# Experts' down weights laid out with two neighbouring lines of the matrix in each partition

## The chip, the cores and the metric

The kernel runs on one core of one Trainium2 chip. Its time is the device time in microseconds (us) of one launch, and a version is judged by the median of its runs. All data are float32.

## What is computed

Two transformer blocks follow each other over 256 tokens of width 1024. The first block has two layers; the second of these ends in a mixture of experts, which is where the change lies. Cut to that part, the reference is:

```python
N_EXPERTS, TOP_K, FFN_EXPERT, MOE_BLOCK = 8, 2, 3584, 128

def moe_swiglu(x, w_router, w1, w3, w2):
    logits = jnp.einsum('nd,de->ne', xf, w_router)
    top_logits, top_idx = lax.top_k(logits, TOP_K)
    gates = jax.nn.softmax(top_logits, axis=-1)
...
    def expert_block(args):
        xb, e = args
        h = jax.nn.silu(xb @ w1[e]) * (xb @ w3[e])
        return h @ w2[e]
```

Each of the eight experts has two up matrices `w1[e]` and `w3[e]` of 1024 x 3584 and a down matrix `w2[e]` of 3584 x 1024. A block of up to 128 tokens (`xb`) meets each expert. In `h @ w2[e]` the sum runs over the 3584 lines of `w2[e]`; the order in which these lines are added is free, as long as line r of the matrix meets column r of `h`.

## The kernel before

**The ring of weights.** All weights stream from the chip's memory through `ring_data`, a ring of 6 slots (`RING`, L33) of 128 partitions x 8 KB, so 1 MB a slot. SyncE (SP) issues the transfers in the order of use, two of 512 KB for each slot, and before each slot it waits until TensorE has used up the slot that lay there (`ring.used`, L716). For each slot that has landed, ScalarE (ACT) rounds the 2048 values of each partition to the format of the fast float32 matmul (`weights_hi`, `e_high`, L2124), VectorE (DVE) subtracts that from the original (`weights_lo`, `e_low`, L2443), and TensorE (PE) makes three products from them: high by high, low by high, high by low. ACT and DVE work three slots ahead of PE (`Wide.LEAD`, L245).

**A turn.** One turn is one expert, 42 slots in a fixed order (`Wide.TURN`, L244): the hidden width of 3584 is cut into chunks of 1024, 1024, 1024 and 512 columns; a chunk takes 8 up slots (4 for the last) and 4 down slots (2 for the last), and the first chunk of the next expert is computed in the turn before (`next`). There are eight turns here: 336 slots, of which 8 x 14 = 112 are down slots. The loop over turns and the lists of slots are the same for SP (`turn_of`), ACT, DVE and PE (`turn`).

**An up slot** holds 128 lines of `w1` and 128 of `w3`, 1024 columns each: every partition gets a run of 4 KB from each (L720). For the last chunk it holds 256 lines of 512 columns, in runs of 2 KB. **A down slot** holds 256 lines of `w2`, each 1024 columns or 4 KB long. Before the change the first transfer brings lines 0 to 127 of the 256, one to each partition, and the second brings lines 128 to 255 (L718 to L720). So partition p holds lines p and 128 + p, and the runs are 4 KB long over all 128 partitions.

**The matmuls.** `up_slot` (L1485, L1486, L1489) and `down_slot` (L1512, L1513, L1517) each issue 12 matmuls of 128 x 512. Line f of the two in a partition meets `ehT[:, 2m + f]` (L1512, L1513), which is the transposed hidden activation: `eh`, 128 tokens x up to 1024 columns, is turned in blocks of 128 x 128 by `turn_h` (L1473), and block q holds columns 128q to 128q + 127. ACT and DVE copy the turned blocks out of PSUM (L2147, L2907). `turn_h` is called four times a turn, with 8, 8, 8 and 4 blocks.

In the rows, `ring_data<-in_moe_w` is a transfer of the experts' weights, `weights_hi` and `weights_lo` are the two halves of a split, and `hT_hi`, `hT_lo` are the turned activations. `arena` is a large buffer in which many tiles lie, `eh` among them. L195 is the line that issues the transfers of all other weights.

Of the kernel before, what the change touches and what calls it, by code (L numbers as in the profile page):

```python
# [14 lines left out]
P = 128  # L15
# [12 lines left out]
CHUNK = 64  # L28
FFN = 2816
E, FE = 8, 3584  # L30
# [257 lines left out]
def cols(ap, c, w):  # L288

    return ap[:, c:c + w].rearrange("(k p) c -> p k c", p=P)  # L290


def two_block_kernel(nc, a, out):

    CO, CONST_W = constant_offsets()
    with ExitStack() as ctx:
# [28 lines left out]
        def sem(name):  # L325

            if name not in S:
                S[name] = ctx.enter_context(nc.semaphore(name))
            return S[name]
# [3 lines left out]
        def bk(i, *dims):  # L333

            n = int(np.prod(dims))
            v = bank[i][:, 0:n]
            if len(dims) == 2:
                v = v.rearrange("p (a b) -> p a b", a=dims[0])
            if len(dims) == 3:
                v = v.rearrange("p (a b c) -> p a b c", a=dims[0], b=dims[1])  # L340
            return v
# [7 lines left out]
        def const(name, k=0, w=None):  # L349
            o, width = CO[name]  # L350
            w = w or width
            return consts[:, o + k * w:o + (k + 1) * w]

        ident, ones, half = const("ident"), const("ones"), const("half")
# [266 lines left out]
        esil, eh = (t.rearrange("p a j c -> p (a j c)") for t in bufs1[:2])  # L621
        ehT_hi, ehT_lo = (t.rearrange("p a q t -> p (a q t)").rearrange("p (k t) -> p k t", k=DT) for t in bufs1[2:])

        def e_slot(at):
            return (n_moe + at) % RING
# [34 lines left out]
        def _(sp):  # L660
# [51 lines left out]
            w1, w3, w2 = (a[k].rearrange("o e d f -> (o e d) f") for k in ("moe_w1", "moe_w3", "moe_w2"))  # L712

            def expert_slot(kind, c, m, e, at, more):

                sp.wait_ge(ring.used, n_moe + at + 1 - RING + more)  # L716
                slot, loaded = ring_data[:, e_slot(at), :], ring.loaded[e_slot(at)]
                if kind == "down":  # L718
                    src = w2[bass.ds(e * FE + 1024 * c + 256 * m, 256), :].rearrange("(f p) d -> p f d", p=P)
                    parts = [(slot.rearrange("p (f d) -> p f d", f=2)[:, i:i + 1, :], src[:, i:i + 1, :]) for i in range(2)]  # L720
                elif c < 3:
                    parts = [(slot[:, 1024 * i:1024 * i + 1024], w[bass.ds(e * D + P * m, P), 1024 * c:1024 * c + 1024]) for i, w in enumerate((w1, w3))]
                else:
                    parts = [(slot[:, 1024 * i:1024 * i + 1024].rearrange("p (k c) -> p k c", k=2),
                              w[bass.ds(e * D + 2 * P * m, 2 * P), 3072:3584].rearrange("(k p) c -> p k c", p=P)) for i, w in enumerate((w1, w3))]
                for d, r in parts:
                    sp.dma_start(d, r).then_inc(loaded, 16)

            def turn_of(it, is_last):
                for s, (kind, c, m) in enumerate(Wide.slots(is_last)):  # L730
                    expert_slot(kind, c, m, (it + (kind == "next")) % E, e_first + s, it * MOE_LOADS)

            for m in range(e_first):
                expert_slot("up", 0, m, 0, m, 0)
# [14 lines left out]
            for m, (c, w, kind) in enumerate(PROJ2):  # L749
                n = N_PROJ2 + m  # L750
                src = cols(a["w_in_2"][0], c, w) if kind != "ki" else None
                if kind == "ki":
                    src = tuple(cols(a["w_in_2"][0], C_KI, HD) for _ in range(2))
                if kind == "kvw":
                    src = (cols(a["w_in_2"][0], C_KV, P), cols(a["w_in_2"][0], C_KI + HD, IH))
                ring2.load(sp, n, ring2.slot(n)[:, 0:8 * w].rearrange("p (k c) -> p k c", k=DT), src)
            for t in range(GATE_SLOTS):
                c, half = C_G + 512 * (t // 2), t % 2
# [6 lines left out]
            for m in range(4):  # L765
                d, rows = m // 2, slice(512 * (m % 2), 512 * (m % 2) + 512)
# [215 lines left out]
        def _(pe):  # L982
# [440 lines left out]
            def moe():  # L1423
                for j in range(TT):
                    for k in range(DT):
                        if j == 0 and k % 2 == 0:
                            pair_arrived(5, k // 2)
                        i = mm(bank[4][:, E * j:E * j + E], actT[:, k, P * j:P * j + P], router_sb[:, k, :], start=k == 0, stop=k == DT - 1)
# [41 lines left out]
                def turn_h(c):  # L1470

                    for q in range(Wide.WIDTHS[c] // P):
                        i = nc.tensor.transpose(bk(6 + q // 4, 4, P)[:, q % 4], eh[:, P * q:P * q + P], ident)  # L1473
                    i.then_inc(sem("moe_hT_psum"), 1)

                def up_slot(c, m, at, split):
# [43 lines left out]
                def turn(it, is_last):  # L1520
                    for s, (kind, c, m) in enumerate(Wide.slots(is_last)):
# [7 lines left out]
                        if part == ("up", 1, 1):  # L1529
                            turn_h(0)  # L1530
# [8 lines left out]
                        if part == ("up", 2, 1):  # L1539
                            pe.wait_ge(sem("y_added"), it * 4 + 4)  # L1540
                            turn_h(1)
# [9 lines left out]
                        if part == ("up", 3, 1):  # L1551
                            pe.wait_ge(sem("pgT_ready"), it + 2)
                            pe.wait_ge(sem("gslot_ready"), it + 1)
                            turn_h(2)
# [1738 lines left out]
```

## Time and profile before

| What | us |
|---|---|
| Median of three runs (lowest to highest) | 2177.38 (2173.64 to 2178.76) |
| Profiled execution, its own time | 2174.22 |
| Its span, first to last instruction | 2172.4 |
| PE busy in the span | 2119.5 (98%) |
| DVE busy | 1595.0 (73%) |
| ACT busy | 1215.9 (56%) |
| Mean rate of all transfers | 250 GB/s |

The span is cut into stages by the work: two mixers and a dense feed-forward part up to some 550 us, the experts from there to some 1557 us, and the second block after that. The hardware profiler's records say for every engine when it worked and for every idle time what ended it. Matmuls overlap each other in the records, so a group's mean duration is longer than the step from one start to the next. "Share of DMA" is the part of the time in which the core's 16 transfer engines had a packet in work.

### The profile page before, as it was taken

To read this page: it belongs to the slowest core of one execution; us is meant where nothing else is said; L and a number is where in the kernel's file an instruction comes from. 1 tells how busy PE (TensorE), PEld (TensorE's weight loads), DVE (VectorE), ACT (ScalarE), POOL (GpSimd) and SP (SyncE) were. 2 spreads that over 40 slices of the span, in tenths; PEclk is the share of its full clock that TensorE was granted. 3 is DMA by queue.
4 is the path that set the end of the run, shared out by engine and by line. 5 is a ranking of instruction groups with operands and counts; after the bars stand their busy time and mean duration, and the time that the engine had idled before them with its cause. 6 is when DMAs were issued, how large, how long until landed. Compare 5 with 4: busy or idle time off the path is not lost.

```text
span 2172.4 us, 31475 instructions
## 1 busy us (share of the span) xinstructions
PE 2119.5 (98%) x11887; PEld 1770.4 (81%) x11887; DVE 1595.0 (73%) x1654; ACT 1215.9 (56%) x1204; POOL 171.3 (8%) x240
## 2 busy tenths in 40 slices
PE   8999999999899999999999999999999999999998
PEld 7987888898778788888888888888788887877886
DVE  3677454577788989989898989989866539776453
ACT  4254443415467777777777777777664423664442
POOL 1200000310200000000000000000166010000000
PEclk9999999999999999999999999999999999999999
DMA  9224555422589999999999999999846564435552
GB/s 353 70 98 165 186 186 184 142 66 93 177 325 373 351 371 375 357 377 360 372 362 371 360 376 367 363 375 362 317 155 192 183 182 156 155 107 173 180 188 78
DMA packets 244114, 542.21 MB, mean 250 GB/s; under 512 B 20182, under 2 KB 122624, under 8 KB 243648
## 3 DMA queue, kind: packets, MB, share of 16 engines
q1 hardware_dynamic: 238608, 521.37, 66.5%
q0 software_dynamic: 4448, 13.79, 2.4%
q10 hardware_dynamic: 976, 5.91, 0.7%
q8 instruction: 57, 0.93, 0.2%
q14 instruction: 25, 0.20, 0.0%
HBM read 538.64 MB, written 2.36 MB: 249 GB/s over the span
## 4 chain that ended last, share of the span: by engine, by line
PE 83%; DVE 10%; issue 3%; ACT 2%; DMA 2%; DVEq 0%; SPq 0%; ACTq 0%
PE bank L1334 9%; PE bank L1335 9%; PE bank L1336 9%; PE bank L1489 7%; PE bank L1485 7%; PE bank L1486 7%; PE bank L1060 6%; PE bank L1512 4%; PE bank L1513 4%; PE bank L1517 4%; DVE weights_lo L2443 2%; PE bank L1058 2%; PE bank L1647 2%; DMA ring_data<-in_moe_w 1%; PE bank L1473 1%
## 5 line engine op out<-in xcount | busy, mean ns | idle before, releaser
L2443 DVE TENSOR_TENSOR weights_lo<-ring_data,weights_hi 128x2048 fp32r<-128x2048 f32 x336 | 760.0, 2288 | 84.4 <-ACT weights_hi L2124 83.2
L2124 ACT ACTIVATE weights_hi<-ring_data 128x2048 fp32r<-128x2048 f32 x336 | 639.0, 1919 | 178.6 <-DMA ring_data<-in_moe_w 178.1
L1485 PE MATMUL bank<-weights_hi,xg_hi 128*128 128x512 f32 x896 | 352.5, 393 | 2.6 <-DVE arena L2901 2.6
L1486 PE MATMUL bank<-weights_hi,xg_lo 128*128 128x512 f32 x896 | 349.8, 390 | 0.0
L2438 DVE TENSOR_TENSOR weights_lo<-ring_data,weights_hi 128x2048 fp32r<-128x2048 f32 x98 | 228.2, 2358 | 49.3 <-ACT weights_hi L1899 49.3
L1489 PE MATMUL bank<-weights_lo,xg_hi 128*128 128x512 f32 x896 | 240.2, 390 | 0.5 <-DVE weights_lo L2443 0.5
L1335 PE MATMUL bank<-weights_lo,xT_hi 128*128 128x512 f32 x584 | 229.5, 393 | 0.0
L1334 PE MATMUL bank<-weights_hi,xT_hi 128*128 128x512 f32 x520 | 206.2, 397 | 1.6 <-issue 0.6
L1336 PE MATMUL bank<-weights_hi,xT_lo 128*128 128x512 f32 x520 | 203.1, 391 | 0.0
L1485 PEld LDWEIGHTS bank<-weights_hi,xg_hi 128*128 128x128 f32 x896 | 168.6, 188 | 37.1 <-issue 3.0
L1489 PEld LDWEIGHTS bank<-weights_lo,xg_hi 128*128 128x128 f32 x896 | 168.5, 188 | 36.3 <-DVE weights_lo L2443 1.0
L1486 PEld LDWEIGHTS bank<-weights_hi,xg_lo 128*128 128x128 f32 x896 | 168.7, 188 | 34.3
L1899 ACT ACTIVATE weights_hi<-ring_data 128x2048 fp32r<-128x2048 f32 x98 | 183.9, 1916 | 0.0
L1512 PE MATMUL bank<-weights_hi,hT_hi 128*128 128x512 f32 x444 | 174.4, 393 | 1.2 <-DVE hT_lo L2907 1.2
L1513 PE MATMUL bank<-weights_hi,hT_lo 128*128 128x512 f32 x444 | 172.9, 389 | 0.0
L1866 ACT ACTIVATE arena<-bank 128x384 f32<-128x384 f32 (+5 forms) x130 | 62.8, 502 | 169.1 <-PE bank L1060 57.4
L2459 DVE TENSOR_TENSOR hT_lo<-bank,hT_hi 128x256 fp32r<-128x256 f32 x66 | 24.9, 419 | 158.3 <-ACT hT_hi L1910 158.3
L1910 ACT ACTIVATE hT_hi<-bank 128x256 fp32r<-128x256 f32 x66 | 21.8, 381 | 208.3 <-PE bank L1355 208.3
L1060 PE MATMUL bank<-actT,ring_data 128*128 128x256 f32 x608 | 135.1, 381 | 0.0
L1335 PEld LDWEIGHTS bank<-weights_lo,xT_hi 128*128 128x128 f32 x584 | 111.0, 190 | 22.2
L1060 PEld LDWEIGHTS bank<-actT,ring_data 128*128 128x128 f32 x608 | 114.5, 190 | 16.5 <-issue 0.4
L1517 PE MATMUL bank<-weights_lo,hT_hi 128*128 128x512 f32 x444 | 118.8, 389 | 0.0
(522 smaller groups left out, 3184.0 us busy)
## 6 DMA issues: line engine op xcount, KB each, us to landing
ring_data<-in_moe_w SPq DMA_DIRECT2D x672, 512.0 KB, 4.4
ring_data<-in_ffn_w_in SPq DMA_DIRECT2D x88, 512.0 KB, 4.5
ring_data<-in_w_in SPq DMA_DIRECT2D x71, 512.0 KB, 4.3
ring_data<-in_ffn_w SPq DMA_DIRECT2D x66, 512.0 KB, 4.0
ring_data<-in_ffn_w_out SPq DMA_DIRECT2D x44, 512.0 KB, 4.0
ring_data<-in_w_out SPq DMA_DIRECT2D x24, 512.0 KB, 4.6
ring_data<-in_w_in SPq DMA_DIRECT2D x8, 396.0 KB, 4.0
ring_data<-in_w_in SPq DMA_DIRECT2D x8, 390.0 KB, 5.4
```

The source lines that it names most:

```text
L1060: i = mm(bk(b, 2, T)[:, g], wt[:, k, P * g:P * g + P], actT[:, k, :], start=k == 0, stop=k == DT - 1)
L1334: mm(o, x_hi, w_hi, start=start, stop=False, **kw)
L1335: mm(o, x_hi, w_lo, start=False, stop=False, **kw)
L1336: return mm(o, x_lo, w_hi, start=False, stop=stop, **kw)
L1485: mm(o, xg_hi[:, k, :], e_hi(at)[:, r], start=k == 0, stop=False)
L1486: mm(o, xg_lo[:, k, :], e_hi(at)[:, r], start=False, stop=False)
L1489: i = mm(bank[2 * part + q][:, :], xg_hi[:, k, :], e_lo(at)[:, r], start=False, stop=k == DT - 1)
L1512: mm(o, ehT_hi[:, 2 * m + f, :], w_hi[:, f, cd], start=first and f == 0, stop=False)
L1513: mm(o, ehT_lo[:, 2 * m + f, :], w_hi[:, f, cd], start=False, stop=False)
L2124: nc.scalar.activation(e_hi(at), ring_data[:, e_slot(at), :], ACT.Copy).then_inc(ring.hi_done, 1)
L2438: v.tensor_tensor(f.lo_slot(f.n0 + at), w, f.hi_slot(f.n0 + at), ALU.subtract).then_inc(f.ring.lo_done, 1)
L2443: v.tensor_tensor(e_lo(at), ring_data[:, e_slot(at), :], e_hi(at), ALU.subtract).then_inc(ring.lo_done, 1)
```

## The change

The 256 lines of a down slot still come in two transfers of 512 KB. The first now brings lines 0 to 127 to partitions 0 to 63, two neighbouring lines to each, and the second brings lines 128 to 255 to partitions 64 to 127. Partition p then holds lines 2p and 2p + 1, which lie next to each other in memory, so each partition's data is one run of 8 KB. To match, `turn_h` turns, of each pair of blocks (256 columns), first the even columns and then the odd ones, reading `eh` with a step of two columns. `CHUNK` is 64. The matmuls, their number and their operands' shapes stay as they were.

```diff
                 if kind == "down":
-                    src = w2[bass.ds(e * FE + 1024 * c + 256 * m, 256), :].rearrange("(f p) d -> p f d", p=P)
-                    parts = [(slot.rearrange("p (f d) -> p f d", f=2)[:, i:i + 1, :], src[:, i:i + 1, :]) for i in range(2)]
+                    rows = [bass.ds(e * FE + 1024 * c + 256 * m + P * i, P) for i in range(2)]
+                    parts = [(slot[CHUNK * i:CHUNK * i + CHUNK, :], w2[r, :].rearrange("(p f) d -> p (f d)", f=2)) for i, r in enumerate(rows)]
...
                     for q in range(Wide.WIDTHS[c] // P):
-                        i = nc.tensor.transpose(bk(6 + q // 4, 4, P)[:, q % 4], eh[:, P * q:P * q + P], ident)
+                        pair = eh[:, 2 * P * (q // 2):2 * P * (q // 2) + 2 * P].rearrange("t (p f) -> t f p", f=2)
+                        i = nc.tensor.transpose(bk(6 + q // 4, 4, P)[:, q % 4], pair[:, q % 2], ident)
```

## Rows read from the trace of the kernel before

**Rows 1.** The page: busy time of engines, and the span in 40 slices

```profile
PE 2119.5 (98%) x11887; PEld 1770.4 (81%) x11887; DVE 1595.0 (73%) x1654; ACT 1215.9 (56%) x1204; POOL 171.3 (8%) x240
...
DMA  9224555422589999999999999999846564435552
GB/s 353 70 98 165 186 186 184 142 66 93 177 325 373 351 371 375 357 377 360 372 362 371 360 376 367 363 375 362 317 155 192 183 182 156 155 107 173 180 188 78
```

**Rows 2.** Stretches of one turn each: busy us by engine, PEclk, DMA share, GB/s

```profile
1093.00:1214.00 121.00, 120.81 (x555) 100.08 (x554) 109.15 (x73) 88.91 (x62) 2.04 (x1) 1.00 0.98 367
1214.00:1336.00 122.00, 121.80 (x559) 100.92 (x558) 109.76 (x73) 89.84 (x65) 2.05 (x1) 1.00 0.98 367
```

**Rows 3.** All waits of PE in the experts' stage, 576 to 1557 us: us, times, longest

```profile
PE bank L1463 <- DVE arena L2895: 3.6, 7, 1.7
...
PE bank L1485 <- DVE arena L2901: 2.6, 1, 2.6
...
PE bank L1443 <- DVE arena L2853: 1.9, 1, 1.9
...
PE bank L1512 <- DVE hT_lo L2907: 1.2, 1, 1.2
...
PE bank L1489 <- DVE weights_lo L2443: 0.5, 1, 0.5
```

**Rows 4.** Waits for transfers and for slots, 720 to 1550 us (ACT, then SP)

```profile
ACT weights_hi L2124 <- DMA ring_data<-in_moe_w: 151.4, 174, 3.1
...
SPq L727 <- PE bank L1489: 347.3, 191, 4.5
SPq L727 <- PE bank L1517: 163.4, 94, 2.6
```

**Rows 5.** Timeline of PE: two down slots and the start of an up slot

```profile
1006.75 0.39 PE L1512 MATMUL bank<-weights_hi,hT_hi 128*128 128x512 f32 x1
...
1009.47 0.39 PE L1512 MATMUL bank<-weights_hi,hT_hi 128*128 128x512 f32 x1
...
1012.19 0.39 PE L1485 MATMUL bank<-weights_hi,xg_hi 128*128 128x512 f32 x1
```

**Rows 6.** DMA view, 700 to 1540 us: packets; queue: packets, MB, share; issues

```profile
DMA packets 91838, 308.39 MB, mean 367 GB/s; under 512 B 9405, under 2 KB 9405, under 8 KB 91830
...
q1 hardware_dynamic: 90678, 304.10, 96.2%
...
ring_data<-in_moe_w SPq DMA_DIRECT2D x581, 512.0 KB, 4.4
```

**Rows 7.** DMA view, 1575 to 1760 us: dense weights in runs of mostly 1 KB

```profile
q1 hardware_dynamic: 26100, 32.01, 52.6%
```

**Rows 8.** DMA view, 1767 to 1775 us: transfers onto 16 partitions each (L967)

```profile
q0 software_dynamic: 501, 1.23, 79.6%
...
arena<-toep POOLq DMA_DIRECT2D x8, 128.0 KB, 4.6
```

**Rows 9.** Line L1473, the transposes: ns min/median/max, first and last start

```profile
L1473 PEld LDWEIGHTS bank<-consts_sb,arena x224: 138/140/142, 612.6 to 1551.1; 128*128 128x128 f32 x112
L1473 PE MATMUL bank<-consts_sb,arena x224: 270/272/273, 612.9 to 1551.2; 128*128 128x128 f32 x112
```

**Rows 10.** Chain that ended last, in order of time: eight transposes and what follows

```profile
1014.17 0.91 PE bank L1489 x4
1015.08 0.87 PE bank L1473 x8
1015.95 0.23 PE bank L1485
```

**Rows 11.** The page: packets of the whole span by their size

```profile
DMA packets 244114, 542.21 MB, mean 250 GB/s; under 512 B 20182, under 2 KB 122624, under 8 KB 243648
```

## The prediction

> **What bounds the kernel now.** I read the page first. PE is busy for 98% of the span, and the slices show a block from about 550 to 1557 us in which the transfer engines are busy as well, at 351 to 377 GB/s [rows 1]. That block is the experts' stage, the only one that the change touches. Next come the stretches of one turn each: 121 us with PE busy for 120.81, at the full clock (the row's 1.00, so 2.4 GHz), and the 16 transfer engines busy for 0.98 of it at 367 GB/s [rows 2]. Two resources are full at once. Which of them sets the pace is told by the waits. PE waits in the whole stage for 3.6 + 2.6 + 1.9 + 1.2 + 0.5 = 9.8 us, and only the last of these, 0.5 us, is a wait for a split of weights [rows 3]. SP, which issues the transfers, waits 347.3 + 163.4 us for PE to give slots back, and ACT waits 151.4 us in 174 waits for transfers to land [rows 4]. So PE is the pacer: it asks for a slot every 2.72 us (two down slots start at 1006.75 and 1009.47, the next slot at 1012.19) [rows 5], and with its other matmuls a turn of 42 slots takes about 121.4 us, 2.89 us a slot. The transfers keep up, but with next to nothing to spare: 1 - 0.98 of 121 us is 2.4 us a turn, some 20 us over eight turns [rows 2]. That is the number on which the case turns. A cheaper transfer can win almost nothing; one that costs more than 20 us in sum makes the transfers the bound.
>
> The sum is made against the profiled execution, 2174.2 us with a span of 2172.4. The median of the three runs is 3.2 us above it (0.15%), and I add these 3 us at the end.
>
> **What a slot costs the transfer engines now.** Between 700 and 1540 us the hardware queue moved 304.10 MB with 96.2% of the engines' time [rows 6]. That is 808 us for 304.10 / 1.0486 = 290 slots, or 2.79 us a slot, 376 GB/s while busy.
>
> **The edits, part by part.**
>
> *Longer runs.* A down slot had 256 runs of 4 KB and gets 128 of 8 KB. The fixed price of a packet can be had from two rows. In the experts' stage a packet of 3354 bytes on average took 808 x 16 / 90678 = 142.6 ns of an engine [rows 6]; in the dense stage, 1226 bytes took 0.526 x 185 x 16 / 26100 = 59.7 ns [rows 7]. The line through both has 0.039 ns a byte and 12 ns a packet. So 8 KB in one packet costs 331 ns against 343 in two: 3.5% off, 0.10 us a down slot, 11 us of the engines' time over 112 slots. The page counts 244114 - 243648 = 466 packets of 8 KB and more already [rows 11], so I take it that such a run goes as one packet; if it is cut into two, this gain is nothing.
>
> *64 partitions a transfer instead of 128.* No row shows a large transfer onto 64 partitions, so its price is bounded. Lower end: a byte costs what it costs now. Upper end: half the partitions take in data at half the rate, and as the two transfers of a slot are issued one behind the other, nothing makes it up: 2 x 2.79 = 5.57 us a slot. Nearest is the stretch from 1767 to 1775 us, in which loads onto 16 partitions each went through the software queue: 1.23 MB with 79.6% of 8 us, or 193 GB/s while busy [rows 8], against 376. The engines were as busy, and moved a byte 1.95 times slower, with an eighth of the partitions. An eighth is three halvings; the cube root of 1.95 is 1.25 for one halving. Part of the 1.95 may come from shorter runs there (512 bytes and 1 KB; by the line above, runs of these sizes would cost 1.33 times as much a byte as 4 KB, which leaves 1.47, or 1.14 a halving), but the row counts 2.4 KB to a packet, so they don't seem to be paid one by one. I take 1.25: 3.48 us a down slot, 0.70 more than now.
>
> The Trainium skill has a rule that speaks against this edit (SBUF — State Buffer, Door 1: The DMA port swizzle): partitions 0 to 63 reach only 8 of the 16 ports on the transfers' side, and it gives 196 GB/s for 64 partitions at 1 MiB. By that a slot would take 5.35 us. It gives 104 GB/s for 16 partitions; the trace has 193 while busy [rows 8], so here transfers onto different partitions must overlap, which the rule's full price leaves out.
>
> *The transposes.* Their number stays at 224, and `eh` is now read with a step of 8 bytes. Eight take 0.87 us on the chain, 0.109 each [rows 10], while one weight load takes 140 ns and one matmul 272, overlapped [rows 9]. No row has a strided operand. Lower end: no difference. Upper end: the pace doubles, 224 x 0.109 = 24 us, all on PE's path. I take nothing, since the operand has the same 128 columns and the same bytes; the 24 us stay for a rival.
>
> *What does not move.* SP issues the same 672 transfers with the same waits; ACT, DVE and PE have the same instructions on the same slots. A landed slot is complete only when both transfers are in, as before, so half a slot landing early helps nobody. These edits cost nothing because none is made.
>
> **The sum.** A down slot costs the transfer engines 0.70 - 0.10 = 0.60 us more. Over 112 down slots that is 67 us; 20 us of it fill the idle time of the engines, and the rest, 47 us, becomes waits of PE, since six slots of ring and a lead of three can shift a shortage within a turn, but not one that returns in every turn. 2174 + 47 = 2221, with the 3 us: **2224 us**, 2.1% slower. What is late next is `weights_hi`: ACT waits longer for the second half of a slot, and DVE and PE stand behind it.
>
> **The rivals.**
>
> *The half rate in full (slower by much).* For it: each engine serves the two transfers of a slot in turn, so all 16 can stand on the same half at once. At 5.57 us a slot the stage pays 112 x 2.78 - 20 = 292 us: 2469. With half of the best rate of a slice, 377 / 2 = 188 GB/s [rows 1], it comes to the same 5.57. Against it: the 193 GB/s onto 16 partitions [rows 8] are already more than half the partitions would then be allowed. A chance of 0.17. The Trainium skill is on its side (DMA: Bandwidth & Descriptors, Rules for kernel authors): two transfers to disjoint halves of the partitions serialize, and one over all 128 is better. By its 196 GB/s the result would be 2174 + 112 x 2.56 - 20 + 3 = 2444, an estimate from that page's figure.
>
> *No change.* Two transfers in flight, one on each half, share the partitions between them, and engines that drift apart by more than one transfer (32 KB, 1.4 us at this rate) are never on the same half. Then a down slot costs up to 2.79 + 20/112 + 0.10 = 3.07 us unseen, a factor of 1.10 before the longer runs' gain. For it: SP runs ahead, so several transfers are queued (4.4 us from issue to landing, three times a transfer's own 1.4) [rows 6], and PE has no waits for transfers now. The lower reading of rows 8, 1.14, lies just above the point. Time: 2177. A chance of 0.27.
>
> *Faster.* If partitions don't matter, the 11 us of the longer runs give the transfers slack of 31 us instead of 20. It decides only from where PE waits for weights, and these are 0.5 us, plus at most the 2.6 and 1.2 us behind DVE, whose splits would come earlier [rows 3]: 4.3 us at best, 2173 against the median. Its price is at the bound of what can be told. A chance of 0.08 for more than that bound, part of it for waits that the profile of one execution doesn't show.
>
> *The strided reads cost.* Up to 24 us on PE's path, 2201, where the transfers keep pace. Against: nothing but the missing row. A chance of 0.05 on its own.
>
> **How the numbers follow.** The forecast has 0.43: partition count costs something, but not all. With the half rate (0.17) and the strided reads (0.05), slower has 0.65; same 0.27; faster 0.08. A measurement of this kernel can tell 0.2%, some 4 us, from no change. The forecast's own range is from factor 1.14 (3.18 - 0.10 = 3.08 us, +13 us: 2190) up to where it meets the half rate, say a factor of 1.8 (5.02 - 0.10 = 4.92 us, +219 us: 2396). The range of 8 in 10 runs from 2168, below the best of the faster case, to 2400; left out are the half rate in full, 0.17, and a little of faster.
>
> **What would show it.** In the changed profile the experts' turns should last about 127 us, the DMA share should be 1.00 in them, PE's busy share should fall to about 0.95, and `weights_hi L2124 <- DMA` should grow. PE should show waits behind L2124 or L2443 that add up to about 50 us. The packets of the span should fall by 112 x 128 = 14336; if they don't, runs are cut. L1473 should keep 0.109 us a transpose on the chain. The forecast is wrong if turns stay at 121.4 us (drifting engines), or if the rate falls towards 190 GB/s while down slots arrive (the half rate), or if PE's new time stands at L1473.

## The result and the profile after

The changed kernel takes 2369.76 us (median of 6 runs, 2354.36 to 2375.37) against 2177.81 before. The ratio is 1.0869, with a 95% interval of 1.084 to 1.0899: slower by 192 us. The direction was forecast; the size, 47 us, was a quarter of it. The profiled execution took 2375.37 us with a span of 2373.5.

The page of the changed kernel, busy times and the 40 slices, then the packets; these answer to [rows 1] and [rows 11]:

```profile
PE 2191.4 (92%) x11887; PEld 1790.5 (75%) x11887; DVE 1597.3 (67%) x1654; ACT 1217.4 (51%) x1204; POOL 172.2 (7%) x240
...
DMA  9226555234999999999999999999975555525552
GB/s 331 73 72 211 188 191 163 75 107 125 289 292 311 294 312 316 280 343 307 302 318 278 321 299 300 319 279 320 317 205 168 190 186 163 188 77 168 184 187 89
DMA packets 229778, 542.21 MB, mean 228 GB/s; under 512 B 20182, under 2 KB 122624, under 8 KB 214976
```

The same bytes are moved, in 244114 - 229778 = 14336 packets fewer, exactly 112 x 128: a run of 8 KB does go as one packet. The stages ahead of the experts and behind them look as before. In the experts' stage the engines are as busy as they were, but move 278 to 343 GB/s in a slice where they had moved 351 to 377.

A slice mixes two kinds of slot, so stretches were chosen in which slots of one kind were arriving. The first four follow each other, with down slots in the second and the fourth; the other four are stretches of up slots from the next 150 us. The line by itself is from the kernel before. Columns as in [rows 2]:

```profile
1042.00:1056.00 14.00, 10.20 (x40) 7.57 (x39) 12.50 (x9) 12.01 (x12) 0.00 (x0) 0.88 1.03 418
1064.00:1080.00 16.00, 15.38 (x68) 12.39 (x67) 12.38 (x10) 7.37 (x6) 0.00 (x0) 1.00 1.02 221
1084.00:1102.00 18.00, 18.00 (x84) 14.99 (x83) 17.44 (x10) 14.29 (x9) 0.00 (x0) 1.00 1.04 420
1104.00:1120.00 16.00, 14.56 (x65) 11.40 (x65) 8.59 (x4) 6.74 (x6) 0.00 (x0) 1.00 1.01 217
...
1152.00:1170.00 18.00, 18.00 (x83) 14.86 (x82) 15.81 (x10) 13.39 (x8) 0.00 (x0) 1.00 1.02 385
1184.00:1202.00 18.00, 13.79 (x55) 10.42 (x54) 15.47 (x15) 15.57 (x13) 0.00 (x0) 0.91 1.03 377
1225.00:1245.00 20.00, 19.77 (x89) 15.61 (x88) 15.94 (x11) 14.41 (x9) 0.00 (x0) 1.00 1.03 354
1268.00:1276.00 8.00, 6.57 (x27) 4.73 (x26) 6.62 (x7) 6.47 (x6) 0.00 (x0) 1.00 1.05 408
```

```profile
1052.00:1060.00 8.00, 8.00 (x41) 6.71 (x40) 6.23 (x4) 6.01 (x6) 0.00 (x0) 1.00 1.02 416
```

The last two columns tell the case. The share of DMA is full in all eight stretches of the changed kernel, but the rate is 217 or 221 GB/s while down slots arrive and 354 to 420 while up slots do. A down slot therefore takes 1.0486 MB / 219 GB/s = 4.79 us: that is the change's cost. The up slots cost about what they did. The first two stretches of them, at 418 and 420 GB/s, are the fastest, 2.50 us a slot, and the expectations of e5 and e6 below take these 2.50 us for the price of every slot. The later ones have 385, 377 and 354 GB/s, which is 2.72 to 2.96 us, on both sides of the 2.79 us from before (408 GB/s is the rate of the last chunk's slots, in runs of 2 KB); and the kernel before reached 416 GB/s in a stretch too. What makes one stretch faster than another is not known. It is not how many transfers are queued: in the stretch of 354 GB/s they took 11.1 us from issue to landing, and in the kernel before, from 1048 to 1060 us, 5.6.

Who waited, 576 to 1760 us, PE's own longest waits and those of ACT and DVE; compare [rows 3] and [rows 4]:

```profile
ACT weights_hi L2125 <- DMA ring_data<-in_moe_w: 442.2, 286, 4.8
DVE weights_lo L2444 <- ACT weights_hi L2125: 282.2, 218, 4.4
...
PE bank L1513 <- ACT weights_hi L2125: 48.7, 43, 3.2
PE bank L1457 <- DMA lnp<-token_rows,row_of: 38.5, 7, 6.1
...
PE bank L1486 <- DVE arena L2902: 21.3, 8, 3.0
...
PE bank L1518 <- DVE weights_lo L2444: 10.4, 50, 0.2
```

PE waits at the down slots (L1513) for the high parts, and ACT for the landing. The second line of PE is a passenger of the same traffic: the gather of the next expert's token rows (L926) goes to the same 16 engines as the weights. On the chain that ended last it is there four times, each time for 14.8 to 15.0 us, once from 1129.01 for 14.96 us. And PE's busy time grew by 72 us with no matmul added. A part of this is the clock: after such waits PE's matmuls run at half speed for a while, as the chain around that gather shows:

```profile
1129.01 14.96 DMA lnp<-token_rows,row_of
1143.98 0.04 issue
1144.02 1.97 PE bank L1457 x8
1145.99 0.43 PE bank L1513
1146.41 0.43 PE bank L1514
...
1148.42 0.23 PE bank L1513
1148.64 0.23 PE bank L1514
```

The matmul of 0.23 us takes 0.43 there (1.2 GHz instead of 2.4), and the stretch from 1042 us above has a granted clock of 0.88 where PE worked for only 10.20 of 14 us. Over the whole span the mean granted clock fell from 0.991 to 0.973, so the time lost to it grew by at most 0.027 x 2373.5 - 0.009 x 2172.4 = 45 us; the rest of the 72 was not traced. Neither the gather nor the clock sets the time, for the transfer engines are full throughout; they are what a stage bound by transfers looks like from PE.

### The profile page after: what moved, and what is told of

It is laid out like the page before. It is cut to its first block, busy times and chain, and to the rows that moved or that the text cites. A ratio compares the mean times of both kernels' runs of the same rounds, so it can differ in the third digit from the quotient of the medians.

```text
span 2373.5 us, 31475 instructions
## 1 busy us (share of the span) xinstructions
PE 2191.4 (92%) x11887; PEld 1790.5 (75%) x11887; DVE 1597.3 (67%) x1654; ACT 1217.4 (51%) x1204; POOL 172.2 (7%) x240
## 2 busy tenths in 40 slices
DMA packets 229778, 542.21 MB, mean 228 GB/s; under 512 B 20182, under 2 KB 122624, under 8 KB 214976
## 4 chain that ended last, share of the span: by engine, by line
PE 64%; DMA 19%; DVE 10%; ACT 3%; issue 3%; SPq 1%; DVEq 0%; POOLq 0%; ACTq 0%
DMA ring_data<-in_moe_w 16%; PE bank L1334 8%; PE bank L1336 8%; PE bank L1335 8%; PE bank L1060 6%; PE bank L1490 5%; PE bank L1486 5%; PE bank L1487 5%; DVE weights_lo L2444 3%; DMA lnp<-token_rows,row_of 3%; ACT weights_hi L2125 2%; PE bank L1058 2%; PE bank L1518 2%; PE bank L1648 2%; PE bank L1513 1%
## 5 line engine op out<-in xcount | busy, mean ns | idle before, releaser
L1486 PE MATMUL bank<-weights_hi,xg_hi 128*128 128x512 f32 x896 | 359.1, 401 | 21.3 <-DVE arena L2902 21.3
L1487 PE MATMUL bank<-weights_hi,xg_lo 128*128 128x512 f32 x896 | 355.8, 397 | 0.0
L1513 PE MATMUL bank<-weights_hi,hT_hi 128*128 128x512 f32 x444 | 188.0, 423 | 58.6 <-ACT weights_hi L2125 48.7
L1514 PE MATMUL bank<-weights_hi,hT_lo 128*128 128x512 f32 x444 | 180.4, 406 | 0.0
L1513 PEld LDWEIGHTS bank<-weights_hi,hT_hi 128*128 128x128 f32 x444 | 88.3, 199 | 96.3 <-ACT weights_hi L2125 68.5
L1518 PE MATMUL bank<-weights_lo,hT_hi 128*128 128x512 f32 x444 | 127.4, 409 | 10.4 <-DVE weights_lo L2444 10.4
```

The costliest lines, as they stand in the source:

```text
L1486: mm(o, xg_hi[:, k, :], e_hi(at)[:, r], start=k == 0, stop=False)
L1487: mm(o, xg_lo[:, k, :], e_hi(at)[:, r], start=False, stop=False)
L1513: mm(o, ehT_hi[:, 2 * m + f, :], w_hi[:, f, cd], start=first and f == 0, stop=False)
```

## The experiments

The theories at the start: **A**, the partitions that a transfer reaches set its rate; **B**, runs or packets of 8 KB are slow; **C**, PE pays for the strided transposes. The first four kernels ran on one chip; before had a median of 2178.72 us there.

### e1: the new layout, one line a transfer

```diff
-                    rows = [bass.ds(e * FE + 1024 * c + 256 * m + P * i, P) for i in range(2)]
-                    parts = [(slot[CHUNK * i:CHUNK * i + CHUNK, :], w2[r, :].rearrange("(p f) d -> p (f d)", f=2)) for i, r in enumerate(rows)]
+                    src = w2[bass.ds(e * FE + 1024 * c + 256 * m, 256), :].rearrange("(p f) d -> p f d", f=2)
+                    parts = [(slot.rearrange("p (f d) -> p f d", f=2)[:, i:i + 1, :], src[:, i:i + 1, :]) for i in range(2)]
```

> The layout and the strided transposes of the changed kernel, but each of the two transfers brings one line to all 128 partitions, in runs of 4 KB. Theory A (the rate is set by how many partitions one transfer reaches): the down slots come at the old rate, time 2178 us, within 0.3%. Theory B (a run or packet of 8 KB is what is slow): also 2178. Theory C (PE pays for reading eh with a step of two): above 2195, with L1474 slower than 0.109 us a transpose on the chain.

Measured: 2191.08 us, ratio 1.006 (1.0041 to 1.0079). The 192 us are gone, but 12 are left: outside the 0.3% of theories A and B, and short of theory C's 2195. From the first to the last transpose of the stage it takes 1566.0 - 617.8 = 948.2 us against 938.3 before, so 10 us of them lie in this stage.

### e2: the old layout, in halves

```diff
-                    parts = [(slot.rearrange("p (f d) -> p f d", f=2)[:, i:i + 1, :], src[:, i:i + 1, :]) for i in range(2)]
+                    halves = [slice(CHUNK * i, CHUNK * i + CHUNK) for i in range(2)]
+                    parts = [(slot.rearrange("p (f d) -> p f d", f=2)[r], src[r]) for r in halves]
```

(against the kernel before, with its transposes)

> The old layout and the old transposes, but transfer i brings both lines of partitions 64i to 64i + 63, so 64 partitions a transfer in runs of 4 KB. Theory A: down slots at 217 to 221 GB/s as in the changed kernel, 2370 us within 1%. Theories B and C: 2178 us.

Measured: 2371.62 us, ratio 1.0895 (1.0819 to 1.0971). This is the changed kernel's time with none of its long runs and none of its strided transposes. A stretch of down slots and the queue's row from 700 to 1540 us:

```profile
1001.00:1008.00 7.00, 7.00 (x25) 5.60 (x25) 3.07 (x2) 4.11 (x4) 0.00 (x0) 0.74 1.05 221
...
q1 hardware_dynamic: 74564, 252.88, 101.3%
```

The changed kernel moved 253.84 MB in that window, this one 252.88. B and C can't be the cause of the 192 us.

### e3: 64 partitions a transfer, but every other one

```diff
-                    rows = [bass.ds(e * FE + 1024 * c + 256 * m + P * i, P) for i in range(2)]
-                    parts = [(slot[CHUNK * i:CHUNK * i + CHUNK, :], w2[r, :].rearrange("(p f) d -> p (f d)", f=2)) for i, r in enumerate(rows)]
+                    src = w2[bass.ds(e * FE + 1024 * c + 256 * m, 256), :].rearrange("(p f) d -> p (f d)", f=2)
+                    parts = [(slot[i:P:2, :], src[i:P:2, :]) for i in range(2)]
```

> The changed kernel, but transfer i brings the runs of 8 KB to the partitions i, i + 2, i + 4 and so on: still 64 partitions and 8 KB a run, but spread over all 128. Theory A in the form that the number of partitions counts: 2370. Theory A in the form that it is the half, 0 to 63 or 64 to 127, that counts: 2178 to 2200. Theory B: 2370.

Measured: 2182.12 us, ratio 1.0023 (1.0012 to 1.0034). The transfers have the same number, size, run length and count of partitions as in the changed kernel; which partitions they are differs, and with it which lines of the matrix come together, and 188 us are gone. The number of partitions is not what counts. Nor are the lines: each transfer of the kernel before brought the same 128 lines as the changed kernel's. A stretch of 100 us:

```profile
1000.00:1100.00 100.00, 100.00 (x458) 83.26 (x458) 86.78 (x53) 72.08 (x50) 2.03 (x1) 1.00 0.98 366
```

### e4: one transfer of 1 MB

```diff
-                    parts = [(slot[i:P:2, :], src[i:P:2, :]) for i in range(2)]
+                    parts = [(slot[:, :], src)]
...
-                    sp.dma_start(d, r).then_inc(loaded, 16)
+                    sp.dma_start(d, r).then_inc(loaded, 32 // len(parts))
```

(against e3)

> The changed kernel, but a down slot comes in one transfer of 1 MB over all 128 partitions in runs of 8 KB. Theory A: 2170 to 2178 us, as PE is the bound again and the longer runs can at most take PE's few waits for weights; the share of DMA in a turn falls from 0.98 to about 0.97. Theory B: 2370.

Measured: 2179.40 us, ratio 0.9997 (0.9981 to 1.0014). With the whole layout of the change and both its edits, but all 128 partitions in one transfer, the kernel is as fast as before, and no faster (1.4 us above the expected range): PE is the bound again. Here are the transposes of the kernel before and of this one, 550 to 1557 us, and eight of this one's on the chain, against 0.87 us in [rows 10]:

```profile
L1473 PEld LDWEIGHTS bank<-consts_sb,arena 128*128 128x128 f32 x224 | 26.3, 139 | 4.2
...
L1474 PEld LDWEIGHTS bank<-consts_sb,arena 128*128 128x128 f32 x220 | 31.1, 205 | 2.4
...
1020.10 0.95 PE bank L1474 x8
```

The strided operand is the one that is loaded as weights, and its load takes 205 ns instead of 139, half of it more. On the path that is 0.010 us a transpose, 2.2 us for 224. Theory C had a cause but no size. e1 and e4 differ only in how the bytes are fetched, and e1 writes its slots in the same 4 KB runs over 128 partitions as the kernel before, so e1's extra belongs to the reads: 128 pieces of 4 KB, 8 KB apart in memory, instead of one stretch. Why such reads are dearer was not tried.

### e5 and e6: only some down slots in halves

The kernel of e4, but for the chunks named:

```diff
-                    parts = [(slot[:, :], src)]
+                    parts = [(slot[r, :], src[r, :]) for r in ((slice(0, CHUNK), slice(CHUNK, P)) if c in (3,) else (slice(0, P),))]
```

(e5; e6 has `c in (0,)`)

> Only the 2 down slots of the last chunk come in halves of 64 partitions, the other 12 of a turn in one transfer over 128; a slot in halves costs the engines 4.79 us (1.0486 MB at 219 GB/s). Theory S (the busy share tells the slack: 2.4 us a turn, 2.79 us for a whole slot): 2 x 2.0 - 2.4 = 1.6 us a turn too much, about 2190 us. Theory L (a transfer in a full queue costs 2.50 us a slot, 420 GB/s, so the slack is 10 us a turn or more, although the engines look busy): 2 x 2.29 us are absorbed, 2178 to 2182 us.

> Only the 4 down slots of chunk 0 in halves. A turn of the changed kernel is 24 x 2.50 + 4 x 2.72 + 14 x 4.79 = 138 us, and 9.3 us more that these do not explain. Theory L with that remainder: 10 whole down slots at 2.50 and 4 at 4.79 give 124.4 us a turn, 3 more than PE's 121.4, so 2202 us. Theory S: 4 x 2.0 - 2.4 = 5.6 us a turn, 2223 us.

Measured, with before at 2178.23 us: e5, with two slots a turn in halves, 2216.84 us, ratio 1.018 (1.0163 to 1.0197); e6, with four, 2192.19 us, ratio 1.0077 (1.0052 to 1.0101). Both theories fell, on e5 above all: the smaller change costs more than twice the larger. Its 38.6 us are 4.8 a turn, more than the engines' extra work of 2 x (4.79 - 2.79) = 4.0 (4.6 with 2.50 for a whole slot), so nothing is absorbed; e6 pays 1.7 us a turn of 8.0. PE's waits in e5, 576 to 1760 us:

```profile
PE bank L1486 <- DVE arena L2902: 14.5, 8, 3.1
PE bank L1463 <- DVE arena L2896: 11.3, 8, 2.3
PE bank L1513 <- DVE hT_lo L2908: 8.5, 1, 8.5
```

They are waits not for weights but for what DVE does for the expert at its end and the next one's start (L2902 is the product of the two up parts, L2896 the sum into the output). The same three were 2.6, 3.6 and 1.2 us before [rows 3]. The first two now come eight times each; the 8.5 us are a single wait. DVE takes its work in a fixed order, so a late slot in front of these would make them late. That is read from the waits, and was not tested by moving DVE's work.

### e7 and e8: the order and the size of the pieces

e7 sends the upper half first in every other down slot (`parts = parts[::-1] if m % 2 else parts`). e8 cuts a slot into four transfers of 256 KB, lower and upper half in turn, and counts the first two on a second semaphore for which ACT waits too:

```diff
+                    src = w2[bass.ds(e * FE + 1024 * c + 256 * m, 256), :].rearrange("(p f) d -> p f d", f=2)
+                    dst = slot.rearrange("p (f d) -> p f d", f=2)
+                    parts = [(dst[CHUNK * i:CHUNK * i + CHUNK, f:f + 1, :], src[CHUNK * i:CHUNK * i + CHUNK, f:f + 1, :]) for f in range(2) for i in range(2)]
```

> The changed kernel with the order of the two halves turned round in every other down slot, so that two transfers onto the same half follow each other. If engines do run ahead into the other half, longer stretches on one half leave less of that: slower than 2370 by 10 us or more. If all 16 engines stay on one half at a time whatever the length: 2370 within 1%.

> The changed kernel with four transfers a down slot, 256 KB each, lower half and upper half in turn (one line of a pair each, runs of 4 KB). An engine has 16 KB of each instead of 32, so it takes less of a lead to be on the other half. If drift lets the halves work together: 2250 to 2340 us, and over 240 GB/s in the down slots. If the engines stay together: 2370 within 1%, 217 to 221 GB/s.

Measured: e7 2373.87 us, ratio 1.0901 (1.0839 to 1.0963); e8 2315.23 us, ratio 1.0632 (1.0596 to 1.0668). A stretch of down slots of each, e7 and then e8:

```profile
1001.00:1010.00 9.00, 7.88 (x32) 6.75 (x33) 3.91 (x2) 5.28 (x5) 0.00 (x0) 0.81 1.01 213
```

```profile
1043.00:1056.00 13.00, 13.00 (x59) 10.76 (x58) 10.00 (x8) 5.38 (x3) 0.00 (x0) 1.00 1.04 245
```

By its time e7 can't be told from the changed kernel, and of its two values it met "2370 within 1%"; e8 met the value for halves that work together. So the halves do work together a little, and more so with smaller pieces: 213, 219 and 245 GB/s with 1 MB (mostly), 512 KB and 256 KB on one half at a time. If each change of half saves a fixed time d over a plain rate r, then 0.524 / r - d = 2.39 us and 0.262 / r - d = 1.07 give r = 199 GB/s and d = 0.25 us, and 1 MB would come at 208. This is an estimate from two rates.

### e9: eighths

As e8, with `for h in (0, 512)` over half lines: eight transfers of 128 KB.

> As e8, but eight transfers of 128 KB a down slot (runs of 2 KB), lower and upper half in turn. Theory O (transfers onto alternate halves overlap for a fixed time at each change of half, about 0.25 us, from 219 GB/s with 512 KB and 245 with 256 KB): 0.41 us a transfer, some 310 GB/s, and 2215 to 2250 us. Theory N (what e8 gained has another cause, as its runs of 4 KB or a chance): 240 to 250 GB/s, 2310 to 2330 us. SP needs 0.33 us an issue, 2.7 us a slot, which is below 3.3.

Measured: 2354.54 us, ratio 1.0816 (1.0786 to 1.0845), so neither value. Two stretches while down slots arrive:

```profile
1000.00:1006.00 6.00, 5.46 (x22) 3.54 (x21) 3.93 (x2) 3.92 (x5) 0.00 (x0) 1.00 1.06 279
1056.00:1080.00 24.00, 23.35 (x103) 18.99 (x103) 18.99 (x15) 10.56 (x7) 0.00 (x0) 1.00 0.69 214
```

With a full queue the rate rises to 279 GB/s, in the direction of theory O if not to its 310. But that lasts only as long as transfers are in stock. Then the engines are busy for 0.69 of the time: SP can't issue fast enough. I had counted 0.33 us an issue; the median of all 1344 in this kernel is 0.468 us, and with what lies between two issues six of them take 3.81 us here:

```profile
1059.57 3.81 SPq L731 DMA_DIRECT2D ring_data<-in_moe_w  x6
```

That is 0.64 us each, 5.1 us for the eight of a slot, more than the 4.79 us of the changed kernel's. A new bound took the place of the old one.

### e10 and e11: two down slots a turn, elsewhere

As e5, with the condition `c == 1 and m < 2` (e10) and `c == 2 and m < 2` (e11).

> As e5, two down slots a turn in halves, but the first two of chunk 1, in the middle of the turn. Theory P (the slack depends on the place: DVE has the gather, scatter and products to do around the end of a turn, and e5 put its 4.6 us a turn there): absorbed, 2178 to 2184 us. Without a role of the place: as e5, 2217.

> As e10, but the first two of chunk 2, 18 slots after those of e10 and eight up slots ahead of those of e5. Theory P: the eight up slots that follow make most of it up, 2180 to 2195 us. Without a role of the place: 2217.

Measured, with before at 2176.84 us: e10 2184.26 us, ratio 1.004 (1.0018 to 1.0061); e11 2186.63 us, ratio 1.0056 (1.0035 to 1.0077). Two slots cost 38.6 us at the end of a turn and 7 and 10 us elsewhere. The place decides how much is absorbed (theory P). e10 lies 0.3 us above its range, e11 within it, and some 2 us of each are the transposes. The expectation of e11 has its place wrong: by the order of a turn (`Wide.TURN`) its two slots come 8 after e10's, not 18, and 12 before e5's, eight of them up slots. Eight up slots follow e5's two as well, at the start of the next turn, so up slots behind the late ones are not what tells e11 from e5.

### e12: quarters of the partitions

Four transfers a down slot, onto partitions 0 to 31, 32 to 63, 64 to 95 and 96 to 127, with the two semaphores of e8:

```diff
+                    parts = [(slot[32 * i:32 * i + 32, :], src[32 * i:32 * i + 32, :]) for i in range(4)]
```

> The changed kernel with four transfers a down slot onto partitions 0 to 31, 32 to 63, 64 to 95 and 96 to 127, in this order, each in runs of 8 KB. Theory H (what counts is the half, below or above partition 64; 32 partitions of a half take in data as fast as its 64): 2370 us within 1%, 210 to 221 GB/s in the down slots. Theory K (the rate goes with the number of neighbouring partitions a transfer reaches): 110 GB/s and some 2900 us.

Measured: 2374.49 us, ratio 1.091 (1.079 to 1.1031). Two stretches of down slots; into the first one some up slots reach:

```profile
1000.00:1008.00 8.00, 7.54 (x30) 6.21 (x31) 2.81 (x2) 2.82 (x2) 0.00 (x0) 0.79 1.01 229
...
1356.00:1370.00 14.00, 13.39 (x59) 10.74 (x58) 10.79 (x7) 5.75 (x3) 0.00 (x0) 1.00 1.01 221
```

Half the partitions again, and no slower (221 and 229 where theory K had 110): theory H. What counts is on which side of partition 64 a transfer lies. e8 and e12 together speak for this rather than for any closed block of partitions: both have four transfers of 256 KB a slot, but e8 changes sides with every one and comes at 245 GB/s, e12 with every second one and comes at 221 to 229. A closed block that lies across partition 64, such as 32 to 95, was not tried.

The Trainium skill says this (SBUF — State Buffer, Door 1: The DMA port swizzle): partitions 0 to 63 reach the same 8 of 16 ports as 0 to 31, with a limit of 218 GB/s. The trace agrees to within a few per cent: 217 to 221 GB/s in the changed kernel, 221 and 229 in e12, and the full rate in e3, whose 64 partitions lie on both sides. The same page says in another section ("Can I just issue two DMAs to hit both halves?") that two transfers onto the two halves gain only 6% over one; here the gain depends on the size, and 279 GB/s were seen with 128 KB.

## Why the prediction was right or wrong

**What bounds the kernel: right.** PE was the pacer and the transfers were next; both showed. e4 confirms that cheaper transfers win nothing.

**The price of a down slot: wrong, and this is the step that failed.** "An eighth is three halvings; the cube root of 1.95 is 1.25 for one halving." The measured factor is 4.79 / 2.79 = 1.72, 2.00 us a slot more instead of 0.60. Two things were wrong with my use of the row [rows 8]. It can't be divided into halvings, for the rate does not fall with each halving: e12 has a quarter of the partitions a transfer and e3 a half, and they go at 221 to 229 GB/s and at the full rate. And I did not look at which 16 partitions these were. The loop around L967 takes them in order, 0 to 15, 16 to 31 and so on, so four transfers in a row, 256 or 512 KB, lie on one side of partition 64. The 193 GB/s were thus no sign against a half rate: they lie below the 219 of one side alone, and may well have been the half rate itself, which no run tested. I used them as an argument against the half rate in full; that rival, with a chance of 0.17, is what happened: its rate was put at 188 GB/s and is 219. The factor 1.72 and the time of 2370 lie within the forecast's own range (up to 1.8 and 2396) and within the stated 2168 to 2400. That is owed to the width of the range, and not to the mechanism: the rate was said to fall with the number of partitions, and it goes with the side.

**The longer runs: right and small.** 14336 packets fewer as worked out. Their 11 us of engine time can't be seen beside the rest; e4, which has them without the halves, is within 0.2% of before. That a run of 8 KB goes as one packet is shown; the time that this saves is not.

**The transposes: right that they don't matter.** 2.2 us instead of the nothing I took, within the bound of 24.

**The slack of the transfers: the smaller error.** I read 2.4 us a turn, 20 in all, from the busy share of 0.98. In the same terms, the extra work was 112 x 2.00 = 224 us and 192 were paid, so 32 were absorbed. With the right price and the slack as forecast, the sum gives 2174 + 224 - 20 + 3 = 2381 us, 11 above the measurement: the price of the slot is nearly all of the miss. The rival's 2469 was 99 us too high, 87 of them because it took 2.78 us more a slot instead of 2.00, and 12 by the slack. But one number for the slack is itself a simplification: two slots a turn cost 38.6 us in one place and 7 in another (e5, e10).

**What would show it.** I named a rate near 190 GB/s while down slots arrive as the sign of the half rate. The sign appeared at 217 to 221. Turns last 147 us (the gather that stands on the chain at 1129.01 stands there again at 1276.06), not the 127 forecast. A share of DMA of 1.00 would have appeared under either theory, and told nothing. PE's waits for the splits (L1513 and L1518) add up to 48.7 + 10.4 = 59 us, near the 50 named, though the loss is four times the forecast: the rest stands in its waits for the gather and for DVE's products and in its longer busy time.

**Still open.** The turn from 1129 to 1276 us adds up if each slot is taken at the rate of its own stretch. 24 up slots at 2.72, 2.78 and 2.96 us and 4 at 2.57 are 78 us. 10 down slots at 4.79 are 48 us. The other 4 come beside the gather. There, from 1132 to 1149 us, the weights' queue (q1) moved 3.30 MB, which is 5.4 us a slot, 22 us for the four:

```profile
q1 hardware_dynamic: 511, 3.30, 88.6%
q0 software_dynamic: 144, 0.52, 13.5%
```

The sum is 148 us, so the 9.3 us that the expectation of e6 left unexplained came from taking 2.50 us for an up slot and 4.79 for every down slot. Why up slots come at 354 GB/s in one stretch and at 420 in another stays open, and so does why e5 pays more than the engines' extra time. That e10 and e11 cost 7 and 10 us, where plain arithmetic had nothing, suggests that the ring of six slots has little stock anywhere.

## What to carry to other kernels

A large transfer should reach both sides of partition 64. If one must be split, split its columns or take every other partition, and not the lower and the upper half, even where that makes the runs longer. Before an unmeasured price is interpolated from a far row, ask what else that row has (here, which partitions its transfers went to, one behind the other), and keep the full effect as a case of its own. Read a rate from several stretches before pricing with it: the 420 GB/s of one stretch were 354 in another. What slack there is depends on the place in the loop: look at what the in-order engines have to do just behind the late item.

## What was not expected of the hardware

- With the transfer engines fully busy, the same runs of 4 KB onto 128 partitions came at 354, 377, 385, 418 and 420 GB/s in different stretches of one kernel, each 14 to 20 us long.
- Transfers onto alternate halves: 213 to 219 GB/s with 512 KB and more on one side at a time, 245 with 256 KB, 279 with 128 KB.
- Reading 128 pieces of 4 KB at a distance of 8 KB costs a little: e1 has 948.2 us between its first and last transpose, and e4, which fetches the same bytes into the same places in one transfer, 940.2.
- A float32 operand of a transpose read with a step of two columns takes 205 ns to load as weights instead of 139.
- SP's issue of a transfer is not a fixed 0.33 us: the median was 0.383 us in the changed kernel and 0.468 with eight transfers a down slot, where one followed the other every 0.64 us.
